# Another layout in DRAM for the dense gates of a product-key expert layer

## The reference, cut to what matters

```python
def peer_ffn(x, w_q, sub_keys, u_table, v_table):
    q = (xt @ w_q).reshape(T, PEER_HEADS, 2, PEER_DK_HALF)
    s = jnp.einsum('thpd,hpnd->thpn', q, sub_keys)
    s1, i1 = lax.top_k(s[:, :, 0], PEER_TOPK)
    s2, i2 = lax.top_k(s[:, :, 1], PEER_TOPK)
    ...
    gates = jax.nn.softmax(top_s, axis=-1)
    ...
        a = jax.nn.gelu(jnp.einsum('cd,ced->ce', xc, u_table[ic]), approximate=False) * gc
        return jnp.einsum('ce,ced->cd', a, v_table[ic])
```

## Time and profile before

| | |
|---|---|
| Time, median of 3 runs | 1678.42 us (1678.31 to 1678.57) |
| The profiled execution | 1678.1 us, span 1676.3 us |
| Share of the span, busy | PE 99%, PEld 88%, DVE 74%, ACT 46%, POOL 46% |
| Granted clock of TensorE | 1.000 of full speed |
| DMA | 433.68 MB, mean 259 GB/s |

### The profile page before, as it was taken

One profiled execution on the slowest core, in us unless ns is written; L12 is line 12 of the kernel. 1 busy time (PEld: TensorE's weight loads), 2 busy tenths in 40 slices (PEclk: granted clock), 3 DMA queues, 4 the chain that ended last, 5 costly groups with the idle time before them and its releaser, 6 DMA issues.

```text
span 1676.3 us, 24605 instructions
## 1 busy us (share of the span) xinstructions
PE 1667.6 (99%) x9035; PEld 1471.9 (88%) x9035; DVE 1233.6 (74%) x2294; ACT 779.4 (46%) x1379; POOL 773.1 (46%) x484
## 2 busy tenths in 40 slices
PE   9999999999999999999999999999999999999998
PEld 7888877788889999999999999998888888888887
DVE  7877636744524799999999476734888888888886
ACT  6533326544212343457777767733433333333334
POOL 4544422344334778865555577775222222232220
PEclk9999999999999999999999999999999999999999
DMA  8322332374345889987778599997999999999993
GB/s 225 101 76 69 109 94 58 94 245 139 113 120 159 284 288 341 337 276 278 292 261 306 203 391 385 392 361 254 367 372 353 369 352 368 356 360 366 353 357 124
DMA packets 258655, 433.68 MB, mean 259 GB/s; under 512 B 14752, under 2 KB 181920, under 8 KB 256872
## 3 DMA queue, kind: packets, MB, share of 16 engines
q1 hardware_dynamic: 202520, 249.11, 45.5%
q0 software_dynamic: 36864, 134.23, 21.1%
q10 hardware_dynamic: 19152, 48.77, 7.9%
HBM read 372.82 MB, written 59.24 MB: 258 GB/s over the span
## 4 chain that ended last, share of the span: by engine, by line
PE 67%; ACT 1%; issue 0%; DVE 0%; ACTq 0%
PE bank L252 21%; PE bank L254 21%; PE bank L253 21%; PE bank L1803 5%; ACT hot L1476 0%; PE bank L1769 0%; ACT L1456 0%; ACT mixbuf L1464 0%; ACT gl L1456 0%; ACT hot L1507 0%; ACT spl_a L243 0%; PE bank L1810 0%; PE x_rows L1769 0%; DVE rows L1760 0%; ACT L1485 0%
## 5 line engine op out<-in xcount | busy, mean ns | idle before, releaser
L247 POOL TENSOR_TENSOR spl_a<-raw,spl_a 128x1024 fp32r<-128x1024 f32 x170 | 409.5, 2411 | 322.5 <-ACT spl_a L243 321.6
L243 ACT ACTIVATE spl_a<-raw 128x1024 fp32r<-128x1024 f32 x295 | 311.9, 1059 | 389.1 <-PE bank L254 376.8
L252 PE MATMUL bank<-act,spl_a 128*128 128x384 f32 (+1 forms) x1216 | 425.7, 350 | 1.1 <-DVE spl_a L247 0.8
L254 PE MATMUL bank<-act,spl_a 128*128 128x384 f32 (+1 forms) x1216 | 417.3, 343 | 0.0
L253 PE MATMUL bank<-act,spl_a 128*128 128x384 f32 (+1 forms) x1216 | 417.1, 343 | 0.0
L252 PE MATMUL bank<-spl_a,aws 128*128 128x512 f32 x768 | 299.0, 389 | 0.0
L254 PE MATMUL bank<-spl_a,aws 128*128 128x512 f32 x768 | 298.8, 389 | 0.0
L253 PE MATMUL bank<-spl_a,aws 128*128 128x512 f32 x768 | 298.8, 389 | 0.0
L1287 POOL DMA_INDIRECT rows<-in_v_tab,expert x128 | 135.5, 1059 | 343.2 <-DVE hot L1695 334.7
L252 PEld LDWEIGHTS bank<-act,spl_a 128*128 128x128 f32 x1216 | 228.5, 188 | 11.4 <-issue 2.9
L253 PEld LDWEIGHTS bank<-act,spl_a 128*128 128x128 f32 x1216 | 228.6, 188 | 8.0 <-issue 1.0
(11 more groups left out here) (321 smaller groups left out, 2375.9 us busy)
## 6 DMA issues: line engine op xcount, KB each, us to landing
raw<-in_u_t SPq DMA_DIRECT2D x128, 512.0 KB, 5.4
raw<-in_v_tab SPq DMA_DIRECT2D x128, 512.0 KB, 7.6
dense_gates<-mixbuf ACTq DMA_DIRECT2D x12, 2048.0 KB, 8.6
mixbuf<-dense_gates SPq DMA_DIRECT2D x32, 768.0 KB, 9.3
gelu_ux<-gl ACTq DMA_DIRECT2D x120, 192.0 KB, 5.3
mixbuf<-gelu_ux SPq DMA_DIRECT2D x30, 768.0 KB, 12.6
raw<-in_w_in SPq DMA_DIRECT2D x43, 512.0 KB, 3.9
raw<-in_w_q SPq DMA_DIRECT2D x16, 512.0 KB, 4.0
```

Of the source, the lines that this page charges most:

```text
L243: eng.activation(spl(n, 0, slice(0, W)), raw[:, s, :], ACT.Copy).then_inc(hi_done, 1)
L247: eng.tensor_tensor(spl(n, 1, slice(0, W)), raw[:, n % RAW, :], spl(n, 0, slice(0, W)).bitcast(F32), ALU.subtract).then_inc(lo_done, 1)
L252: nc.tensor.matmul(out, w_hi, x_hi, start=first, stop=False)
L254: return nc.tensor.matmul(out, w_lo, x_hi, start=False, stop=last)
```

## The change

The DRAM tensor of the dense gates is laid out by partition first, then by group of four chunks, then by token block. The write of one token block still has 2 MB. It is now cut into 128 x 32 = 4,096 runs of 512 bytes in DRAM, where it had 128 runs of 16 KB. The read of four chunks now has 128 runs of 6 KB, where it had 1,536 runs of 512 bytes. The places in SBUF, the number of DMAs, their issuers, their order and all waits stay.

```diff
-    dense_d = nc.dram_tensor("dense_gates", (DT // TB, P, NC * TB), F32, kind="Internal").ap()
+    dense_d = nc.dram_tensor("dense_gates", (P, NC // 4, DT // TB, 4 * TB), F32, kind="Internal").ap()
...
-            sp.dma_start(gates_in[:, half, :, :, :].rearrange("p b c t -> p b (c t)"),
-                         dense_d[:, :, c * TB:(c + 4) * TB].rearrange("b p x -> p b x")) \
+            sp.dma_start(gates_in[:, half, :, :, :].rearrange("p b c t -> p (b c t)"),
+                         dense_d[:, c // 4, :, :].rearrange("p b x -> p (b x)")) \
                 .then_inc(mix_in[half], 16)
...
-                            act_e.dma_start(dense_d[b, :, :], stage[:, b % 2, :, :].rearrange("p c t -> p (c t)")) \
+                            act_e.dma_start(dense_d[:, :, b, :],
+                                            stage[:, b % 2, :, :].rearrange("p (g c) t -> p g (c t)", c=4)) \
                                 .then_inc(stage_stored[b % 2], 16)
```

## The result

The changed kernel takes 1745.05 us (median of 4 runs, 1743.02 to 1750.9), against 1678.37 us before (4 runs). The ratio is 1.040, with a 95% interval of 1.039 to 1.0415. That is 66.7 us slower; the forecast was 29 us slower and its range ended at 1733.

What follows compares the result with a forecast made beforehand. PE was taken as the bound, busy 1667.6 of 1676.3 us. Ten writes, each held 7.4 us less 4.5 of slack, add 29; reads and transfer add 0: 1678.4 + 29 = 1707.5 us, range 1677 to 1733 (forecast's own 1683 to 1733).

Steps and rivals of the forecast that it cites:

- the place, the mechanism and the sign: First stage: ACT's gelu store behind each dense write held about 7.4 us, PE waiting beyond its slack; +29 us, 55%.
- The reads are worth nothing: Second stage: dense reads free 26 us of DMA time, but PE was never late there; priced 0, bounds 0 to -0.3 us.
- Rival (a): ACT's hold is shorter than PE's slack, or its queue takes all 4,096 runs; 1678.4 us or some tenths less; 34%.
- The capacity of 1,700 runs: ACT's queue takes about 1,700 runs, so the next DMA waits until 2,400 of the write's 4,096 have moved.
- The slack: Hold of ACT that costs PE nothing behind a dense write: mean 4.5 us over the ten writes counted.
- (b): Faster: in the second stage a dense read no longer delays the v loads; 1674 us; 3%.
- (d): The dense reads stay in pieces of 512 bytes and SP's queue as before; no number changes, no chance of its own.
- the clock of 1.00: Granted clock in both stretches, dense writes and dense reads; taken as leaving no clock to win back, no term priced.
- the factor of 1.3 on the hold: Stretching of the write's 4.6 us by other queues' transfers; with 1.4 us at the start gives a 7.4 us hold.
- rival (c): Long hold: other transfers keep their 0.63 share and the write starves; 60 to 84 us more, 1750 us; 8%.
- The eighth and the last write: No quads in the step behind them, next thing due a gelu two steps later; left out of the sum, at 0.
- The transfer term: Dense writes at 267 instead of 375 GB/s: 28 us more DMA time in 327 us, share 0.84 to 0.92; cost 0.

Runs made afterwards that it cites:

- e3: Changed kernel with each dense write cut into four DMAs of 1,024 runs, issued one a step over four steps: 1687.72 us, ratio 1.0063.
- e4: Changed kernel with each dense write cut into four DMAs of 1,024 runs, issued directly behind each other: 1752.57 us, ratio 1.045.
- e6: Changed kernel with groups of eight chunks, so each dense write has 2,048 runs of 1 KB: 1686.22 us, ratio 1.0044.
- e8: Changed kernel with the dense writes issued by SP, two steps later, instead of by ACT: 1684.39 us, ratio 1.0036.
- e9: Kernel before, with 7 to 17 extra ACT copies ahead of the gelu store at each dense write, transfers untouched: 1746.91 us, ratio 1.041.
- e2: Kernel before, with only the read changed, to 128 runs of 6 KB; the write as before: 1678.36 us, ratio 0.9999.
- e10: Kernel before, with 10 extra ACT copies at each of the twelve dense writes, transfers untouched: 1721.92 us, ratio 1.026.
- e7: Changed kernel with 16 useless PE products ahead of the quads it waits for, behind ten of twelve writes: 1748.26 us, ratio 1.042.
- e11: Changed kernel with first-stage gathers fetching 2 KB instead of 4 KB for each of 128 rows: 1713.69 us, ratio 1.021.
- e5: Changed kernel with the dense write issued behind the gelu store of its step instead of ahead of it: 1712.03 us, ratio 1.020.

## Why the prediction was wrong

**Right: the place, the mechanism and the sign.** ACT's next DMA is held behind 4,096 runs and PE loses what goes beyond its slack (e3, e4, e6, e8, e9). 1,024 runs at a time pass nearly free, four times 1,024 don't. The reads are worth nothing (e2). Rival (a) fell: the store behind each write took 4.8 to 11 us. The rule that the text had weighed for it, on descriptors given out before their number costs, stands in the section of the Trainium skill (page "DMA: Bandwidth & Descriptors", section "Anatomy of one DMA — SWDGE (gpsimd) path") on DMAs that GpSimd issues. It didn't bear on ACT's queue, and no run here tests it on POOL's.

**Right only in part: the capacity and the slack.** The capacity of 1,700 runs is not a fixed number. The store was taken with 1,851 to 947 runs left at the first seven writes and with 1,187 to 717 at the last five. In e6 it was taken with up to 1,873 left. The slack was read as 4.5 us and was 5.1 (e10) to 5.2 (8.7 us of mean hold over the ten writes, 34.8 us of waiting, in the changed kernel). The reading had counted ACT's work up to the last of the eight scalings, 4.25 us behind the fourth write. PE's first quad needs only four of them: there it starts 3.2 us after ACT is free (865.13 to 868.36), which gives a slack of 5.1 us.

**Rivals (b) and (d).** (b) didn't show, and (d) neither: the reads did get shorter, in flight and in SP's queue, as forecast.

**Wrong, first: the clock.** The text took the clock of 1.00 as one of the things that couldn't be won back, and left out that it can be lost. PE's busy time grew by 21.7 us, some 18.7 of them by the half clock. The growth is 0.5 us for each us of added idle time: 21.7 for 44.8 here, 22.3 for 45.2 in e9, 15.6 for 28.5 in e10. In the other slower kernels, e7 with its added products aside, it was 0.35 (e6, whose trace has no stretch at half clock) to 0.64 (e11). So it is a description of these kernels, and a small part of it isn't the clock's. The term is the largest part of the miss, and with it alone the forecast would have been 1707.5 + 15 = 1722 or so, as e10 measured.

**Wrong, second: the factor of 1.3 on the hold.** The first seven holds had a mean of 7.7 us for the 7.4 forecast. The last five had 11.3. I had taken the other queues' load as one mean over 327 us, and read their effect from writes of 16 KB runs. The load of gathers more than doubles in the last part (e11). By then the other queues did keep half of the engines, as in rival (c), and some 3,150 runs had to move where the forecast had 2,400. At their own pace 2,680 runs, the early number, would have taken 11.3 x 2,680 / 3,150 = 9.6 us, so about half of the growth from 7.7 to 11.3 us is the pace and half the number (an estimate). Over the ten writes that I counted the mean hold was 8.7 us: 10 x 1.3 = 13 us more. The slack, 0.7 us larger than read, took 7 of them back, and PE waited 34.8 us for the scalings where the forecast had 29.

**Wrong, third: the eighth and the last write.** I put them at 0, because no quads follow and the next thing due was a gelu two steps later. It was due too early for a hold of 11.5: PE waited 10.9 us for the two gelus. So the slack there is about 6 us, and even the 7.4 us of the forecast would not have been free: in e6 holds of 7.3 us at these two writes cost 1.0 and 1.4 us. In e10, where they were 6.3 us, PE waited 0.4 us for gelu in all.

29 + 13 - 7 + 11 + 22 = 68, against 66.5 measured in the traces. Rival (c), over 60 us, came nearest, but only the late holds went its way: PE's idle time grew by 45 us, not 66, and the growth of its busy time, mostly the clock's, made up the rest.

**The transfer term** was sized rightly. In the first hold ACT's queue was alone and moved 1.15 MB in 5.6 us at a share of 0.761, which is 270 GB/s at full share, where the text had 267. It did not show in the changed kernel, where PE's waits spread the same bytes over more time: 0.79 in the forecast's own stretch, 761 to 1088 us. Where the same runs went out and little was held (e3), that stretch reads 0.92, as forecast:

```profile
761.00:1088.00 327.00, 326.02 (x2127) 325.19 (x2126) 262.16 (x552) 236.12 (x562) 208.24 (x129) 1.00 0.92 314
```

## What to carry to other kernels

Count the runs of a DMA, not only its bytes, and ask what is the next DMA of the engine that issues it: behind 4,096 runs that next one was held until 1,900 or fewer were left, and with it the engine's arithmetic; behind 1,024 it mostly was not. A scattered write belongs on an engine whose stream has slack (SP here, 6 us instead of 67) or has to be cut and spread over time; cutting alone does nothing. When a change makes PE stand for several microseconds at a time, price the clock too (here PE's busy time grew by about half of the added idle time), and size a hold in the part of the stretch where the other queues are fullest, not by the mean.

## What the runs showed of the hardware that was not expected

- Behind a DMA of 4,096 runs the next DMA of the same engine is held, and the DMA itself is not: in the changed kernel its own instruction took 0.53 to 0.59 us. The next one there was taken with 717 to 1,851 runs left, 5.6 us behind the write at best and, with 4,096 runs in e5, 17.5 at worst. SP's loads were not held meanwhile, nor were ACT's stores where SP issued the write (e8).
- PE's rate after a stand-still: products 0.32 us apart for 3.7 us behind a wait of 5.3 us, then 0.17 again. Waits of 3 to 6.5 us were followed by a stretch at half clock; of three waits of 1.6 to 1.9 us, the first was and the other two were not. In e6 waits of up to 2.6 us left the clock at full.
- PE's busy time grew by about 0.5 us for each us of added idle time, whether ACT was held by its DMA (0.48) or busy with copies (0.49 and 0.55).
